# A two-block model's forward pass, in which the normalised columns get 1,280 bytes a k-tile and the weight tiles lie side by side

## The chip, the cores and the metric

The kernel runs on one core of one Trainium2 chip. The metric is the device time of one execution in microseconds (us), the median of several runs.

## What is computed

The input is 256 tokens of width 2,048. The first block has multi-head attention and a pooling branch, then a feed-forward part with a 3-tap convolution. The second block puts 16 learned tokens ahead, which makes 272 columns (`TOK`; `SEQ` is 256), and has two layers. The even layer multiplies the normalised tokens `u` by one wide matrix, and its parts feed a state-space scan and a 31-tap convolution; both results go through an output projection. The odd layer is neighbourhood attention with its own two projections. Cut to the lines around the change:

```python
h = x + jnp.concatenate([a, m], axis=-1) @ w_out       # block 1
h = h + conv_ffn(rms_norm(h, g), w_up, conv_w, conv_b, w_down)
u = rmsnorm(h, norm_g)                                 # even layer, 272 rows
proj = u @ w_in    # z_a, xs, B, C, dt_f, dt_b, z_b, glu_v, glu_g
y_a = ssd_mixer(...)
y_b = layernorm(conv31(glu_v * sigmoid(glu_g))) ...  * silu(z_b)
h = h + jnp.concatenate([y_a, y_b], axis=-1) @ w_out
u = rmsnorm(h, norm_g)                                 # odd layer
h = h + (neighbourhood_attention(q, k, v, rpb) * silu(z)) @ w_out
return rmsnorm(h, g)[:, 16:]
```

All products are in float32, each made from three fp32r products: weights and activations are split into a high and a low part, and high x high, high x low and low x high are added up in PSUM.

## The kernel before, in words

Activations lie transposed: a k-tile is 128 of the 2,048 features on the partitions by 272 (or 256) token columns. Weights stream from HBM in chunks of 512 KB: SyncE loads a chunk of eight 128 x 128 tiles into one of four `raw` buffers, ScalarE copies it as fp32r into `whi` (`split`, L680 and L682), VectorE or GpSimd subtracts and writes `wlo` (L1642, L1645, L620), and TensorE makes 24 matmuls of it (`product`, L1160 to L1177: three for each k-tile, at L1173, L1174 and L1175). Semaphores `hi_done`, `lo_done` and `chunk_done` count chunks. Each engine has its own program, whose order is written out by hand.

The stages by the name of their weights, with the activations that they read: `pin`, `qkv` and `up` read `th`/`tl` (256 columns, k-tiles 1,024 bytes apart), `mix` and `down` read `fh`/`fl` (the same); `dt`, `xbc`, `ssd` (with `ssd6` and `ssd7`) and `glu` read `xh`/`xl` (272 columns, k-tiles 1,088 bytes apart); `outa` reads `yah`/`yal` and `outb` `ybh`/`ybl` (272 columns, 1,088 bytes); `na` reads `xh`/`xl`, with 272 columns for values and keys and the last 256 for gate and queries; `naout` reads `oh`/`ol` (256 columns, 1,088 bytes apart). In the trace `xh`, `xl`, `th` and `tl` are all named `xhl`, `fh` and `fl` are `fhl`, `oh` and `ol` are `ohl`.

Two things are done about addresses within a partition. From `dt` on, the function `by_lines` (L1154) gives a matmul its columns in another order: four floats of every 64-byte line, then the next four of every line, on both the moving operand and the output. And from `dt` on, `spread` (L289) is true and the eight weight tiles of a chunk don't lie side by side: tile r starts at `r % 4 * GROUP + r // 4 * P` floats (L307), and `GROUP` is 272 floats, so that four pairs of tiles start 1,088 bytes apart, as the k-tiles of the activations do. Before `dt` the eight tiles lie side by side, 512 bytes apart, 64 bytes into the buffer.

Around the change: `rs` are two buffers for the reciprocal roots of the norms (`rs[0]` for `pin` to `qkv` and `dt` to `glu` and the last norm, `rs[1]` for `up` and `na`). `vec` holds all per-feature vectors, the 31-tap weights `conv31` among them; all but its first part are loaded by SyncE during `qkv` (L428). In `glu`, VectorE applies the 31 taps (L2278 to L2290) after the gate's and value's evacuations (L2269, L2270). GpSimd's queue has, before its splits of `glu` (L624), the clamps of the state-space stage and the loads `decay_rows` (L570).

Of the kernel before, what the change touches and what calls it, by code (L numbers as in the profile page):

```python
# [18 lines left out]
P = 128  # L19
D = 2048  # L20
KT = D // P
# [9 lines left out]
GROUP = 2 * P + LINE  # L31
WSLOT = 4 * GROUP
# [39 lines left out]
for _name, _n in (("g_attn", 16), ("g_q", 1), ("g_k", 1), ("rel", 8), ("pool_scale", 8),  # L72
                  ("g_ffn", 16), ("g_even", 16), ("g_odd", 16), ("g_final", 16),
                  ("g_ssd", 16), ("ffn_conv", FT * 8),
                  ("conv5", 32 * 6), ("conv31", 16 * 32), ("ln_g", 16), ("ln_b", 16), ("d_skip", 16),
                  ("dt_bias", 1), ("a_log", 1)):
    VECS[_name] = (_at, _n)
    _at += _n
NVEC = _at
NFIRST = VECS["g_ffn"][0]  # L80

# [32 lines left out]
def program(nc, io):  # L114
    ctx = ExitStack()
    with ctx:
# [27 lines left out]
        vec = at("vec", NVEC)  # L144
        ident = at("ident", P)
        ones = at("ones", P)
        tri = at("tri", 2 * DW, BF16)
        S0 = arena[0]
        sq = at("sq", 2 * TOK)
        nt = at("nt", TOK)  # L150
# [29 lines left out]
        pts = at("pts", 384, F32, U + 1536)  # L180
        sm = at("sm", 8, F32, U + 3072)
# [21 lines left out]
        pad5 = [at(f"pad5{n}", TOK + 4, F32, (s0 + 51712, s0 + 52832, s0 + 54016, U + 2624)[n]) for n in range(4)]  # L203
# [15 lines left out]
        lsq = at("lsq", 2 * TOK, F32, w + 15360)  # L219

        ohl = at("ohl", 2 * KT * TOK, F32R, Y)
        oh, ol = ohl[:, 0:KT * TOK], ohl[:, KT * TOK:2 * KT * TOK]
        cmask = at("cmask", 4 * 2 * NC, F32, w + 17536)
        n0 = Y + 34816
# [63 lines left out]

        def spread(phase, i, j):  # L289

            if isinstance(i, int):
                return chunk(phase, i, j) >= chunk("dt", 0, 0)
            return first(phase, 1) >= first("dt", 1)

        def tiles_of(t, spread_):

            if spread_:
                t = t[:, :].rearrange("p (q m) -> p q m", m=GROUP)[:, :, 0:2 * P]
                return t.rearrange("p q (h n) -> p h q n", n=P)
            return t[:, LINE:LINE + CW].rearrange("p (h q n) -> p h q n", h=2, n=P)  # L300

        def raw_tiles(t):
            return t[:, :].rearrange("p (h q n) -> p h q n", h=2, n=P)

        def wtile(t, r, spread_):

            o = r % 4 * GROUP + r // 4 * P if spread_ else LINE + r * P  # L307
            return t[:, o:o + P]
# [59 lines left out]
        def _(sp):  # L368
# [127 lines left out]
        def _(pool):  # L496
# [118 lines left out]
            def split(phase, i, j, lead=LEAD):  # L615
# [42 lines left out]
        def _(act):  # L658
# [14 lines left out]
            def split(phase, i, j, lead=LEAD):  # L673
# [1936 lines left out]
```

## Time and profile before

| | |
|---|---|
| median of 3 runs | 2375.08 us (2374.9 to 2377.41) |
| the profiled execution, its own time | 2376.99 us |
| its span, first to last instruction | 2375.2 us |
| TensorE matmuls, share of the span | 99%, 20,022 instructions |
| VectorE, ScalarE, GpSimd | 74%, 49%, 25% |
| granted TensorE clock | 0.998 of full speed, mean |
| DMA | 438.55 MB, mean 185 GB/s |

A matmul's recorded duration overlaps the next one's, so its mean tells little of the pace: what counts is how far apart the starts are. In a view by windows, the number after the x counts every instruction that overlaps the window. A matmul here lasts some 280 ns and starts are some 120 ns apart, so about 2.3 of the number were already running when the window began.

### The profile page before, as it was taken

How to read it: one execution, taken by the hardware profiler on the slowest of the kernel's cores; microseconds unless marked ns; L12 is line 12 of the kernel's file. 1: busy time of each engine (PE TensorE's matmuls, PEld its weight loads, DVE VectorE, ACT ScalarE, POOL GpSimd, SP SyncE). 2: the span in 40 equal slices, each digit the busy share in tenths (PEclk: the TensorE clock that was granted, in tenths of full speed). 3: DMA queues.
4: the chain of work that ended last, by engine and by line, in shares of the span. 5: the costliest groups of instructions: out<-in, count | busy, mean ns of one | idle time of the engine just before them, and what ended most of it. 6: DMA issues, size and time to landing. Idle time of an engine off the chain costs nothing.

```text
span 2375.2 us, 55946 instructions
## 1 busy us (share of the span) xinstructions
PE 2352.9 (99%) x20022; PEld 2322.0 (98%) x20022; DVE 1751.0 (74%) x3054; ACT 1173.6 (49%) x1647; POOL 582.4 (25%) x420
## 2 busy tenths in 40 slices
PE   8999999999999999999999999999999999999998
PEld 8999999999999999999999999999999999999997
DVE  6777877777777655589888878888872566666665
ACT  5444455555555444457666643333544444444453
POOL 0230000000000000013423368777777311111100
PEclk9999999999999999999999999999999999999999
DMA  8654666666666666656555545556555555555553
GB/s 281 212 165 143 207 200 200 203 201 201 199 205 197 201 194 195 190 181 198 177 181 169 181 161 177 175 173 192 176 174 175 187 175 161 171 166 177 164 170 133
DMA packets 152419, 438.55 MB, mean 185 GB/s; under 512 B 32324, under 2 KB 47213, under 8 KB 152189
## 3 DMA queue, kind: packets, MB, share of 16 engines
q1 hardware_dynamic: 148844, 424.68, 55.9%
q0 software_dynamic: 3184, 12.14, 1.8%
q8 instruction: 73, 1.20, 0.2%
q10 hardware_dynamic: 288, 0.30, 0.0%
q14 instruction: 30, 0.24, 0.0%
HBM read 434.88 MB, written 11.09 MB: 188 GB/s over the span
## 4 chain that ended last, share of the span: by engine, by line
PE 93%; DVE 4%; ACT 2%; issue 1%; DMA 0%; SPq 0%; DVEq 0%; ACTq 0%
PE bank L1175 29%; PE bank L1173 29%; PE bank L1174 29%; PE bank L1426 1%; DVE wlo L1642 1%; PE bank L1546 1%; PE bank L1536 1%; DVE c L2064 1%; PE bank L1526 1%; PE bank L1397 1%; DMA x<-x_tok 0%; ACT whi L682 0%; PE bank L1553 0%; PE bank L1271 0%; PE bank L1409 0%
## 5 line engine op out<-in xcount | busy, mean ns | idle before, releaser
L1173 PE MATMUL bank<-xhl,whi 128*128 128x256 f32 (+1 forms) x4494 | 1268.7, 282 | 1.2 <-DVE xhl L1713 1.2
L1175 PE MATMUL bank<-xhl,wlo 128*128 128x256 f32 (+1 forms) x4494 | 1261.8, 281 | 0.0
L1174 PE MATMUL bank<-xhl,whi 128*128 128x256 f32 (+1 forms) x4494 | 1257.6, 280 | 0.0
L1173 PEld LDWEIGHTS bank<-xhl,whi 128*128 128x128 f32 x4494 | 843.8, 188 | 4.1 <-DVE xhl L1713 1.5
L1174 PEld LDWEIGHTS bank<-xhl,whi 128*128 128x128 f32 x4494 | 845.8, 188 | 0.7 <-issue 0.2
L1175 PEld LDWEIGHTS bank<-xhl,wlo 128*128 128x128 f32 x4494 | 844.1, 188 | 0.0
L680 ACT CAST whi<-raw 128x1024 fp32r<-128x1024 f32 x420 | 438.7, 1046 | 372.7 <-PE bank L1175 361.9
L1645 DVE TENSOR_TENSOR wlo<-raw,whi 128x1024 fp32r<-128x1024 f32 x364 | 445.4, 1228 | 187.7 <-ACT whi L682 182.8
L682 ACT CAST whi<-raw 128x1024 fp32r<-128x1024 f32 x364 | 381.1, 1052 | 389.3 <-PE bank L1175 368.4
L620 POOL TENSOR_TENSOR wlo<-raw,whi 128x1024 fp32r<-128x1024 f32 x160 | 383.0, 2402 | 122.3 <-ACT whi L680 122.3
L1642 DVE TENSOR_TENSOR wlo<-raw,whi 128x1024 fp32r<-128x1024 f32 x260 | 319.1, 1228 | 108.6 <-ACT whi L680 105.7
L1173 PE MATMUL bank<-fhl,whi 128*128 128x256 f32 x960 | 265.9, 277 | 0.0
L1174 PE MATMUL bank<-fhl,whi 128*128 128x256 f32 x960 | 265.0, 276 | 0.0
L1175 PE MATMUL bank<-fhl,wlo 128*128 128x256 f32 x960 | 265.0, 276 | 0.0
L586 POOL MEMSET pad<- 128x2 f32 x4 | 0.3, 97 | 852.9 <-DVE dta L2019 852.9
L2288 DVE SCALAR_TENSOR_TENSOR bank<-u,vec,bank 128x272 f32<-128x272 f32 x448 | 187.4, 499 | 3.7 <-DVE zt L1656 3.7
L1174 PEld LDWEIGHTS bank<-fhl,whi 128*128 128x128 f32 x960 | 180.3, 188 | 0.0
L1173 PEld LDWEIGHTS bank<-fhl,whi 128*128 128x128 f32 x960 | 180.2, 188 | 0.0
L1175 PEld LDWEIGHTS bank<-fhl,wlo 128*128 128x128 f32 x960 | 180.2, 188 | 0.0
L580 POOL TENSOR_SCALAR ef<-bc,acsr 128x272 f32<-128x272 f32 (+2 forms) x90 | 93.9, 1055 | 175.0 <-PE bank L1426 171.3
L653 POOL TENSOR_TENSOR btm<-btr,cmask 128x160 f32<-128x160 f32 x64 | 46.7, 760 | 345.5 <-DVE nsc L2387 345.2
L695 ACT ACTIVATE sq<-x 128x272 f32 (+1 forms) x64 | 27.6, 432 | 144.0 <-DVE x L1898 144.0
(281 smaller groups left out, 2704.1 us busy)
## 6 DMA issues: line engine op xcount, KB each, us to landing
raw<-w_up SPq DMA_DIRECT2D x176, 512.0 KB, 4.4
raw<-w_na SPq DMA_DIRECT2D x128, 512.0 KB, 3.8
raw<-w_ssm SPq DMA_DIRECT2D x96, 512.0 KB, 3.9
raw<-w_glu SPq DMA_DIRECT2D x96, 512.0 KB, 3.6
raw<-w_down SPq DMA_DIRECT2D x80, 512.0 KB, 4.2
raw<-w_qkv SPq DMA_DIRECT2D x48, 512.0 KB, 4.5
raw<-w_mix SPq DMA_DIRECT2D x32, 512.0 KB, 4.2
raw<-w_outa SPq DMA_DIRECT2D x32, 512.0 KB, 3.8
```

What stands on the lines that cost most here:

```text
L580: ins = G.tensor_scalar(ef[k][0:rows, h * DW + o:h * DW + o + w_], bc[2 * k][0:rows, t0:t0 + w_], acsr[0:rows, c:c + 1], 0.0, SUB, ALU.min)
L620: nc.gpsimd.tensor_tensor(tiles_of(wlo[s], wide), raw_tiles(raw[s]), tiles_of(whi[s], wide).bitcast(F32), SUB).then_inc(sem("lo_done"), 1)
L653: ins = G.tensor_tensor(by_row(btm, (2 * h + b_) * NK, (4, 0)[b_], NC), from_, m_, ADD)
L680: A.copy(tiles_of(whi[s], True), raw_tiles(raw[s])).then_inc(sem("hi_done"), 1)
L682: A.copy(whi[s][:, LINE:LINE + CW], raw[s][:, :]).then_inc(sem("hi_done"), 1)
L695: A.activation(sq[:, k * TOK:k * TOK + TOK], src, ACT.Square).then_inc(sem("sq_done"), 1)
L1173: T.matmul(to_, wh, xh_, start=head, stop=False)
L1174: T.matmul(to_, wh, xl_, start=False, stop=False)
L1175: ins = T.matmul(to_, wl, xh_, start=False, stop=last)
L1642: V.tensor_tensor(tiles_of(wlo[s], True), raw_tiles(raw[s]), tiles_of(whi[s], True).bitcast(F32), SUB).then_inc(sem("lo_done"), 1)
L1645: V.tensor_tensor(wlo[s][:, LINE:LINE + CW], raw[s][:, :], whi[s][:, LINE:LINE + CW].bitcast(F32), SUB).then_inc(sem("lo_done"), 1)
L2288: ins = V.scalar_tensor_tensor(out=out, in0=src, scalar=c, in1=acc_, op0=MUL, op1=ADD)
```

## The change

- The k-tiles of `xh` and `xl` get 320 floats (1,280 bytes, `XW`) for their 272 columns, and both begin one line (64 bytes) into their part of `xhl`. `oh` and `ol` get 256 floats a k-tile instead of 272 and begin three lines in, as `th` and `tl` do. `yah`, `yal`, `ybh`, `ybl` stay as they are.
- `spread` and its helpers go; the eight weight tiles lie side by side in every stage. `by_lines` is applied in the same stages as before.
- To make room: `conv31` leaves `vec` and is loaded by GpSimd's queue into `taps31`, a buffer of its own over dead space of the scan stage, once the first bank of `ssd7` is free. VectorE waits for it ahead of the loop of `glu`. One buffer `rs[0]` serves all norms. `acc`, `nv`, `pts`, `sm` and `pad5[3]` move to other addresses.
- VectorE's residual of `down` has one loop of seven passes where a loop of six and a pass written out stood.

```diff
-GROUP = 2 * P + LINE
-WSLOT = 4 * GROUP
+XW = TOK + 3 * LINE
...
+NKEPT = VECS["conv31"][0]
...
-        rs = [at(f"rs{n}", TOK) for n in range(2)]
-        acc = at("acc", TOK)
-        whi = [at(f"whi{s}", WSLOT, F32R) for s in range(RING)]
-        wlo = [at(f"wlo{s}", WSLOT, F32R) for s in range(RING)]
-        nv = at("nv", TOK)
+        whi = [at(f"whi{s}", CW, F32R) for s in range(RING)]
+        wlo = [at(f"wlo{s}", CW, F32R) for s in range(RING)]
         x = at("x", KT * TOK)
-        xhl = at("xhl", 2 * KT * TOK, F32R)
-        xh, xl = xhl[:, 0:KT * TOK], xhl[:, KT * TOK:2 * KT * TOK]
+        xhl = at("xhl", 2 * KT * XW, F32R)
+        xh, xl = xhl[:, LINE:KT * XW], xhl[:, KT * XW + LINE:2 * KT * XW]
...
+        taps31 = at("taps31", 16 * 32, F32, w + 17536)
+
+        ohl = at("ohl", LINES + 2 * KT * SEQ, F32R, Y)
+        oh, ol = ohl[:, LINES:LINES + KT * SEQ], ohl[:, LINES + KT * SEQ:LINES + 2 * KT * SEQ]
...
-                    sp.dma_start(vec[:, NFIRST:NVEC], io["vecs"][:, NFIRST:NVEC]).then_inc(sem("vec_in2"), 16)
+                    sp.dma_start(vec[:, NFIRST:NKEPT], io["vecs"][:, NFIRST:NKEPT]).then_inc(sem("vec_in2"), 16)
...
+            pool.wait_ge(sem("bank_free"), tile("ssd7", 0, 0) + 3)
+            G.dma_start(taps31[:, :], io["vecs"][:, NKEPT:NVEC]).then_inc(sem("taps31_in"), 16)
             pool.wait_ge(sem("lo_done"), chunk("glu", 0, 0) + (LEAD + RING))
...
-                if spread(phase, i, j + lead):
-                    A.copy(tiles_of(whi[s], True), raw_tiles(raw[s])).then_inc(sem("hi_done"), 1)
-                else:
-                    A.copy(whi[s][:, LINE:LINE + CW], raw[s][:, :]).then_inc(sem("hi_done"), 1)
+                A.copy(whi[s][:, :], raw[s][:, :]).then_inc(sem("hi_done"), 1)
...
-                    wide = spread(phase, i, j)
-                    wh, wl = wtile(whi[s], r, wide), wtile(wlo[s], r, wide)
+                    wh, wl = whi[s][:, r * P:r * P + P], wlo[s][:, r * P:r * P + P]
...
-                product(phase, i, j, j // 2, xh, xl, ktiles(j), TOK, off, n, j % 2 == 0, j % 2 == 1)
+                product(phase, i, j, j // 2, xh, xl, ktiles(j), XW, off, n, j % 2 == 0, j % 2 == 1)
...
-                product("naout", 2, j, j // 2, oh, ol, ktiles(j), TOK, 0, SEQ, j % 2 == 0, j % 2 == 1)
+                product("naout", 2, j, j // 2, oh, ol, ktiles(j), SEQ, 0, SEQ, j % 2 == 0, j % 2 == 1)
...
-            norm(1, rs[1], EPS1)
+            norm(1, rs[0], EPS1)
...
+            dve.wait_ge(sem("taps31_in"), 16)
             with dve.Fori(0, 8) as i:
...
-                        src, c = u31[:, n:n + TOK], vcol("conv31", 32 * m + n, i, 64)
+                        src, c = u31[:, n:n + TOK], ncol(taps31, 32 * m + n, i, 64)
```

## Rows read from the trace of the kernel before

**Rows 1.** The page's part 4, the chain that ended last, by engine.
```profile
PE 93%; DVE 4%; ACT 2%; issue 1%; DMA 0%; SPq 0%; DVEq 0%; ACTq 0%
```
**Rows 2.** What TensorE waited for: us in total, times, longest; the latest-stage entry.
```profile
PE bank L1409 <- ACT cx L709: 1.1, 1, 1.1
```
**Rows 3.** TensorE by windows: us, busy (number), granted clock, DMA share, GB/s.
```profile
400.00:600.00 200.00, 200.00 (x1767) 1.00 0.63 203
...
1384.00:1419.00 35.00, 35.00 (x287) 1.00 0.56 181
1428.00:1660.00 232.00, 232.00 (x1859) 1.00 0.56 179
...
1701.00:1759.00 58.00, 58.00 (x466) 1.00 0.53 168
1761.00:1855.00 94.00, 94.00 (x754) 1.00 0.53 174
```
**Rows 4.** The same view, a window of naout.
```profile
2287.00:2350.00 63.00, 63.00 (x543) 1.00 0.55 175
```
**Rows 5.** TensorE's timeline in outa, 1679.7 to 1699.8 us: start, duration.
```profile
1679.73 0.29 PE L1174 MATMUL bank<-yal,whi 128*128 128x272 f32 x1
...
1699.74 0.28 PE L1175 MATMUL bank<-yah,wlo 128*128 128x272 f32 x1
```
**Rows 6.** TensorE's timeline in the ssd stage, 1157.7 to 1166.9 us.
```profile
1157.72 0.29 PE L1175 MATMUL bank<-xhl,wlo 128*128 128x272 f32 x1
...
1166.84 0.28 PE L1173 MATMUL bank<-xhl,whi 128*128 128x272 f32 x1
```
**Rows 7.** TensorE's timeline in na, a stretch of 272 columns.
```profile
2004.01 0.28 PE L1174 MATMUL bank<-xhl,whi 128*128 128x272 f32 x1
...
2011.24 0.28 PE L1173 MATMUL bank<-xhl,whi 128*128 128x272 f32 x1
```
**Rows 8.** TensorE's timeline in na, a stretch of 256 columns.
```profile
2017.74 0.27 PE L1174 MATMUL bank<-xhl,whi 128*128 128x256 f32 x1
...
2024.80 0.28 PE L1173 MATMUL bank<-xhl,whi 128*128 128x256 f32 x1
```
**Rows 9.** TensorE's timeline where the loop of glu begins.
```profile
1423.59 0.31 PE L1173 MATMUL bank<-xhl,whi 128*128 128x272 f32 x1
1423.74 0.28 PE L1174 MATMUL bank<-xhl,whi 128*128 128x272 f32 x1
```
**Rows 10.** Groups by line and shape on TensorE: number, busy us, mean ns.
```profile
L1173 PE MATMUL bank<-xhl,whi 128*128 128x272 f32 x2064 | 590.3, 286 | 0.0
...
L1173 PE MATMUL bank<-yah,whi 128*128 128x272 f32 x256 | 73.4, 287 | 0.0
...
L1173 PE MATMUL bank<-ybh,whi 128*128 128x272 f32 x256 | 73.1, 286 | 0.0
...
L1173 PE MATMUL bank<-ohl,whi 128*128 128x256 f32 x256 | 71.5, 279 | 0.0
```
**Rows 11.** The page's part 5: the splits of the weights.
```profile
L680 ACT CAST whi<-raw 128x1024 fp32r<-128x1024 f32 x420 | 438.7, 1046 | 372.7 <-PE bank L1175 361.9
L1645 DVE TENSOR_TENSOR wlo<-raw,whi 128x1024 fp32r<-128x1024 f32 x364 | 445.4, 1228 | 187.7 <-ACT whi L682 182.8
L682 ACT CAST whi<-raw 128x1024 fp32r<-128x1024 f32 x364 | 381.1, 1052 | 389.3 <-PE bank L1175 368.4
L620 POOL TENSOR_TENSOR wlo<-raw,whi 128x1024 fp32r<-128x1024 f32 x160 | 383.0, 2402 | 122.3 <-ACT whi L680 122.3
L1642 DVE TENSOR_TENSOR wlo<-raw,whi 128x1024 fp32r<-128x1024 f32 x260 | 319.1, 1228 | 108.6 <-ACT whi L680 105.7
```
**Rows 12.** The tile bc, which GpSimd's queue loads 32 times, 272 KB each.
```profile
DMA to landing us min/median/max: 3.6/5.1/8.7
```
**Rows 13.** VectorE's timeline between the first evacuation of ssd7 and glu.
```profile
1366.83 0.42 DVE L1656 TENSOR_TENSOR nv<-bank,rs 128x272 f32<-128x272 f32 x1
...
1382.89 0.28 DVE L2262 MEMSET bank<- 128x272 f32 x1
```
**Rows 14.** GpSimd's timeline there: its first split of glu's weights.
```profile
1377.77 2.38 POOL L620 TENSOR_TENSOR wlo<-raw,whi 128x1024 fp32r<-128x1024 f32 x1 [25.66 <-ACT whi L680]
```

More of the change, by code:

```diff
@@ L147, in program @@
         tri = at("tri", 2 * DW, BF16)
+        rs = [at("rs0", TOK)]
         S0 = arena[0]
         sq = at("sq", 2 * TOK)
+        acc = at("acc", TOK)
+        nv = at("nv", TOK)
         nt = at("nt", TOK)
@@ L202, in program @@
         dtc = at("dtc", TOK, F32, s0 + 50624)
-        pad5 = [at(f"pad5{n}", TOK + 4, F32, (s0 + 51712, s0 + 52832, s0 + 54016, U + 2624)[n]) for n in range(4)]
+        pad5 = [at(f"pad5{n}", TOK + 4, F32, (s0 + 51712, s0 + 52832, s0 + 54016, V0 + -(-VECS["ffn_conv"][0] // 8) * 32)[n]) for n in range(4)]
         ea = at("ea", 8, F32, s0 + 53952)
@@ L287, in wait_lo @@
             eng.wait_ge(sem("lo_done"), chunk(phase, i, j) + (1 + RING))
[L289 to L308, printed above, removed]
         class Chain:
@@ L741, in first_hi @@
                 act.wait_ge(sem(f"raw_in{j}"), 16)
-                A.copy(whi[j][:, LINE:LINE + CW], raw[j][:, :]).then_inc(sem("hi_done"), 1)
+                A.copy(whi[j][:, :], raw[j][:, :]).then_inc(sem("hi_done"), 1)
             def scaled_hi(q):
@@ L755, in _ @@
             act.wait_ge(sem("raw_first"), 16)
-            A.copy(whi[0][:, LINE:LINE + 2 * P], raw[0][:, 0:2 * P]).then_inc(sem("hi_first"), 1)
+            A.copy(whi[0][:, 0:2 * P], raw[0][:, 0:2 * P]).then_inc(sem("hi_first"), 1)
             act.wait_ge(sem("vec_in"), 16)
@@ L759, in _ @@
             act.wait_ge(sem("raw_in0"), 16)
-            A.copy(whi[0][:, LINE + 2 * P:LINE + CW], raw[0][:, 2 * P:CW]).then_inc(sem("hi_done"), 1)
+            A.copy(whi[0][:, 2 * P:CW], raw[0][:, 2 * P:CW]).then_inc(sem("hi_done"), 1)
             scaled_hi(1)
@@ L1152, in _, with by_lines @@
             pe.sem_inc(sem("chunk_done"), RING)
-            def by_lines(ap, wide):
-                if not wide:
+            def by_lines(ap, phase):
+                if ap.shape[-1] != TOK and phase not in ("na", "naout"):
                     return ap
@@ L1168, in product @@
                     r, o = kt % (4 if phase == "dt" else 8), kt * width + off
-                    wide = spread(phase, i, j)
-                    wh, wl = wtile(whi[s], r, wide), wtile(wlo[s], r, wide)
+                    wh, wl = whi[s][:, r * P:r * P + P], wlo[s][:, r * P:r * P + P]
                     head, last = start and n_ == 0, stop and n_ == len(kts) - 1
-                    to_, xh_, xl_ = (by_lines(a, wide) for a in (out, mh[:, o:o + n], ml[:, o:o + n]))
+                    to_, xh_, xl_ = (by_lines(a, phase) for a in (out, mh[:, o:o + n], ml[:, o:o + n]))
                     T.matmul(to_, wh, xh_, start=head, stop=False)
@@ L1579, in projecting @@
             def projecting(n, n_tile, kts, start=False, stop=False, done=True):
-                product("naout", n // 4, n % 4, n_tile % 2, oh, ol, kts, TOK, 0, SEQ, start, stop,
+                product("naout", n // 4, n % 4, n_tile % 2, oh, ol, kts, SEQ, 0, SEQ, start, stop,
                         {2: bank[2], 3: bank[3]}.get(n_tile), done)
@@ L1615, in last_products @@
                         T.matmul(bank[2][:, META:TOK], ones[:, :], acc[:, META:TOK], start=True, stop=False)
-                    product("naout", i, j, j // 2, oh, ol, ktiles(j), TOK, 0, SEQ, j % 2 == 0,
+                    product("naout", i, j, j // 2, oh, ol, ktiles(j), SEQ, 0, SEQ, j % 2 == 0,
                             j % 2 == 1)
@@ L1902, in landed @@
                     elif gain:
-                        both(tok(x, k, i, 2, 0, TOK), tok(xh, k, i, 2, 0, TOK),
-                             tok(xl, k, i, 2, 0, TOK), vcol(gain, k, i, 2)
+                        both(tok(x, k, i, 2, 0, TOK), tok(xh, k, i, 2, 0, TOK, XW),
+                             tok(xl, k, i, 2, 0, TOK, XW), vcol(gain, k, i, 2)
                              ).then_inc(sem("xs_ready"), 1)
@@ L1944, in residual @@
                     ch.end()
-                    with dve.Fori(1, 7) as i:
+                    with dve.Fori(1, 8) as i:
                         ch.begin(i, 2, 1)
                         body(i)
-                    ch.end(6)
-                    body(7)
-                    ch.end()
+                    ch.end(7)
                 else:
@@ L2279, in tap @@
                         out = c31[:, :] if n == TAPS - 2 else acc_
-                        src, c = u31[:, n:n + TOK], vcol("conv31", 32 * m + n, i, 64)
+                        src, c = u31[:, n:n + TOK], ncol(taps31, 32 * m + n, i, 64)
                         if n == 0:
-                            ins = V.tensor_scalar(out, src, c, vcol("conv31", 32 * m + TAPS, i, 64),
+                            ins = V.tensor_scalar(out, src, c, ncol(taps31, 32 * m + TAPS, i, 64),
                                                   MUL, ADD)
```

52 lines of the change are left out of this document (23 added, 29 removed).

## The prediction

> **What bounds the kernel.** I read the chain first: 93% of it is TensorE [rows 1]. Then TensorE's waits: the largest outside the kernel's start is 1.1 us [rows 2]. So the only thing that can move the time by much is how far apart the starts of the matmuls are, and a nanosecond there counts in full. The windows give that: the length over the number, less the 2.3 that were already running. With 256 columns in plain order (up) it is 200 / 1764.7 = 113.3 ns. With 272 columns it takes one of two values. The first part of glu has 35 / 284.7 = 122.9 ns, the rest of it 232 / 1856.7 = 125.0 ns, the rest of outa 58 / 463.7 = 125.1, outb 94 / 751.7 = 125.1 [rows 3]. The first part of outa has 163 starts in 20.01 us, 122.8 ns [rows 5]; one of three stretches of the scan stage with the same look has 73 in 9.12 us, 124.9 ns [rows 6], and na's 272 columns have 59 in 7.23 us, 122.5 ns [rows 7]. The clock is granted in full in all windows (1.00, the 2.4 GHz level), so it isn't the clock. It isn't the operands either: glu has both paces with the same tiles. The pace turns where something shakes the rhythm: at the entry of glu's loop two starts are 0.15 us apart instead of 0.12 [rows 9], and from there on the pace is the slow one; in outa it turns at an inserted matmul at 1,700 us. I call them the **quick** (122.8) and the **slow** (125.0) pace; they differ by 2.2 ns. In the 256-column stages with reordered columns there is such a spread too: na has 62 starts in 7.06 us, 113.9 ns [rows 8], naout 63 / 540.7 = 116.5 ns [rows 4].
>
> **What decides the pace** the trace doesn't show, but the addresses in the code offer one thing that the change alters: the distance between the moving k-tile and its weight tile, as a remainder by 256 bytes. I take 256 because four lines of 64 bytes is the step after which the old layout repeats. Before, weights begin at remainder 64 and step by 1,088 bytes, the columns at 128 and step by 1,088: the distance is 64 in every k-tile of xh, ya, yb and oh (for the second four weight tiles, 3,840 bytes off, also). For na's 256 columns, which begin 64 bytes later, it is 128; for th and fh it is 192.
>
> **The change, part by part.**
> 1. xh/xl (dt, xbc, ssd, glu, na). Weights now begin at 128 and step by 512, columns at 192 and step by 1,280: the difference of the steps is 768, three times 256. So the distance stays 64 (128 for na's 256 columns). All three matmuls of a k-tile see what they saw. Cost 0 on 3 x 2,064 matmuls of 272 columns [rows 10]. Bounds for what I can't see, that the places themselves matter: down to plain order's 113.3 x 272 / 256 = 120.4 ns, up to 125.0.
> 2. outa and outb, 2 x 768 matmuls (three lines of 256 each [rows 10]). Their columns keep 1,088 bytes, the weights now 512: the distance goes 0, 64, 128, 192 and round again. No row shows that. Bounds: the quick pace, 1,248 matmuls (156 us / 125.0 ns) x 2.2 ns = 2.7 us less; and, since the two 256-column stages that differ in distance and region differ most by 116.5 - 113.3 = 3.2 ns, 1,536 x 3.2 = 4.9 us more. I take 0: the stage already runs at the slow pace, and four distances in turn should average.
> 3. naout, 768 matmuls: from distance 64 to 192, in the same column order. Bounds: 113.3 (up, distance 192, plain order) and 116.5 (now). I take na's 113.9, the nearest in column order with a distance other than 64: 768 x 2.6 = **2.0 us less**.
> 4. The splits. ScalarE's copy takes 1,046 ns spread and 1,052 side by side, VectorE's subtraction 1,228 both ways [rows 11]: 0. GpSimd's takes 2,402 ns and has only the spread form; a chunk in glu lasts 24 x 125 = 3.0 us, and GpSimd waits for ScalarE between splits [rows 11], so 0.6 us more each would be hidden, and less is worth nothing.
> 5. The 31-tap weights. SyncE's load in qkv shrinks by 256 KB; nothing on the path waits for it: 0. GpSimd issues a load of 256 KB after the evacuation that ends at 1366.83 + 0.42 = 1367.3 us; its queue's 272 KB loads land in 5.1 us, at worst 8.7 [rows 12]: at 1372.4, worst 1376.0. VectorE comes to the new wait at 1382.89 + 0.28 = 1383.2 [rows 13]. Slack 7.2 us at worst, cost 0. Behind the load on GpSimd's queue stands its first split, at 1377.77 after 25.66 us of idling [rows 14]: also free. If the cover were gone, behind VectorE's wait stand glu's first evacuations, for which TensorE's banks wait.
> 6. One `rs`: VectorE writes it and reads it in its own order, and no other engine reads it: 0. The moved buffers and the loop of seven passes issue the same instructions: 0.
>
> Sum: -2.0 us. The profiled execution's own time is 2376.99 us for a span of 2375.2, 1.9 above the median, 2375.1; so 2375.0 for that execution and **2373.1 us** for the median. A measurement of this kernel can tell some 0.2%, 4.8 us, from no change, so this is no difference.
>
> **The rivals.**
> - **No place matters.** Then naout keeps 116.5 ns and the median stays 2375.1. For it: glu has both paces with the same addresses. Against: na and naout differ by 2.6 ns in one column order. The Trainium skill, "SBUF — State Buffer", section "Who interferes with whom", is on this side: TensorE has two independent read ports, one for moving columns and one for weights, and never waits on anyone. By it the whole change would be worth nothing; the trace, with 122.9 and 125.0 ns in one stage, shows at least that something unnamed there takes time.
> - **glu falls into the quick pace.** Which pace follows a shake seems to hang on the moment it comes at: in the scan stage three stretches are slow and the others quick. glu from 1423.9 to 1663.5 us is 239.6 us / 125.0 = 1,917 matmuls x 2.2 = 4.2 us less, with naout 6.2: 2368.9. Against: addresses by remainder, order and shake are as before, so the same turn should follow.
> - **The fixed place is better.** Every k-tile of xh now begins at the same remainder, where before it walked by 64 bytes. If that takes the whole 272-column work in xh from about 123.7 on average to between 122.3 and 120.4 ns, 6,192 matmuls give 9 to 20 us: some 2363, with naout. For it: outb's gaps repeat after 12 matmuls, four k-tiles, which is the walk's own length. Against: glu's slow pace repeats after 3 and the quick one after 9, which a walk of 12 would break (these repeats are in the starts to the nanosecond; the printed rows round to ten).
> - **The slow pace spreads** (the side of slower). What now runs quick in xh, about 2,050 of the scan stage, 1,536 of na and 320 of glu, is some 3,900 matmuls; at the slow pace that is 8.6 us more, less naout's 2.0: 2381.7. It decides from about 3,070 such matmuls on (6.8 us, which leaves 4.8 net). For it: every interruption draws anew, and na has two in each of 16 passes. Against: the distances are unchanged, and na's passes all look alike now.
> - **The round of distances in outa and outb** costs its bound of 4.9 us and naout doesn't gain: 2380.0. The late load of the taps is worth a chance of 0.01 only.
>
> **How the numbers follow.** Forecast with no visible difference 0.39 (0.26 as summed, 0.13 no place matters). Faster 0.37: glu quick 0.20, fixed place 0.17. Slower 0.24: slow pace 0.16, outa and outb 0.07, taps 0.01. The range goes down to 2361 (part of the fixed place's 20 us is left out, about 0.08) and up to 2383 (2381.7 and a little; about 0.08 left out, where mishaps add up). The likeliest case's own range is 2370.5 to 2376.
>
> **What would show it.** Right: TensorE still at 93% or so of the chain; up at 113.3 ns; windows in ssd and na at 122.8 and 113.9; glu after its loop's entry at 125.0; naout at 113.9 instead of 116.5; outa and outb between 123 and 127, with gaps that repeat after 12; no wait of VectorE for `taps31`, landed by 1,376 us. Wrong: glu at 122.8 throughout (second rival), any xh stage under 122.5 (third), ssd or na at 125 (fourth), outa and outb over 127, or naout still at 116 or above; and a median under 2370 or over 2380 makes the sum wrong, whichever stage it comes from.

## The result, and the profile after

The changed kernel takes 2361.11 us (median of 4 runs, 2360.02 to 2361.49), the one before 2375.77 (4 runs, 2374.9 to 2377.41): a ratio of 0.9936, 95% interval 0.9923 to 0.995. It is faster by 14.7 us, where 2.0 had been summed, and lies at the very end of the stated range of 2361 to 2383. The two profiled executions stand a little further apart, 17.0 us by their spans (2375.2 and 2358.2 us): the one before lies 1.2 us above its median, the one after, 2360.02 us, 1.1 below.

**Where it went, by stage.** The tile view gives the first and last start of each stage's matmuls. Kernel before:

```profile
L1173 PE MATMUL bank<-fhl,whi x960: 276/276/470, 217.0 to 1026.0; 128*128 128x256 f32 x192
L1426 PE MATMUL bank<-ef,xr x192: 179/286/443, 1085.2 to 1378.3; 128*64 128x272 f32 x64, 128*64 128x144 f32 x64, 128*64 128x16 f32 x64
L1173 PE MATMUL bank<-yah,whi x256: 279/285/485, 1663.9 to 1759.9; 128*128 128x272 f32 x128
L1173 PE MATMUL bank<-ybh,whi x256: 284/286/287, 1760.3 to 1855.9; 128*128 128x272 f32 x128
L1173 PE MATMUL bank<-ohl,whi x256: 274/276/464, 2268.3 to 2362.2; 128*128 128x256 f32 x128
```

Changed kernel, the same view (its lines 1151, 1152 and 1153 are 1173, 1174 and 1175 of before):

```profile
L1151 PE MATMUL bank<-fhl,whi x960: 276/276/470, 217.0 to 1026.0; 128*128 128x256 f32 x192
L1404 PE MATMUL bank<-ef,xr x192: 179/286/443, 1085.0 to 1374.1; 128*64 128x272 f32 x64, 128*64 128x144 f32 x64, 128*64 128x16 f32 x64
L1151 PE MATMUL bank<-yah,whi x256: 280/283/483, 1652.5 to 1747.9; 128*128 128x272 f32 x128
L1151 PE MATMUL bank<-ybh,whi x256: 282/283/382, 1748.3 to 1842.8; 128*128 128x272 f32 x128
L1151 PE MATMUL bank<-ohl,whi x256: 271/277/466, 2252.8 to 2345.2; 128*128 128x256 f32 x128
```

Up to 1026.0 us nothing has moved. From there each stage's length is the difference of two rows (scan stage with dt and xbc to 1378.3, glu to 1663.9, and so on; na from the last start of ybh to the first of ohl, outa and outb likewise):

| | dt to ssd7 | glu | outa | outb | na | naout, end |
|---|---|---|---|---|---|---|
| before, us | 352.3 | 285.6 | 96.4 | 95.6 | 412.4 | 106.9 |
| after, us | 348.1 | 278.4 | 95.8 | 94.5 | 410.0 | 105.4 |
| difference | -4.2 | -7.2 | -0.6 | -1.1 | -2.4 | -1.5 |

So 13.8 of the 17.0 us are in the three stages that read `xh`, which the prediction had put at nothing.

**The pace.** Windows of TensorE (us, busy with the number of instructions, granted clock, DMA share, GB/s):

```profile
400.00:600.00 200.00, 200.00 (x1767) 1.00 0.63 202
1560.00:1592.00 32.00, 32.00 (x269) 1.00 0.55 180
...
1700.00:1740.00 40.00, 40.00 (x327) 1.00 0.49 162
1750.00:1840.00 90.00, 90.00 (x731) 1.00 0.55 180
2275.00:2335.00 60.00, 60.00 (x527) 1.00 0.57 184
```

Less the 2.3 instructions already running, `up` has 200 / 1764.7 = 113.3 ns as before, a stretch within one pass of glu 32 / 266.7 = **120.0 ns** (125.0 before [rows 3]), outa 123.2, outb 90 / 728.7 = 123.5 (125.1 before; this window holds a stop of 0.1 us, and the undisturbed starts are 123.3 apart), naout 60 / 524.7 = 114.4 (116.5 [rows 4]). The clock is 1.00 in all, the 2.4 GHz level. Na's two shapes, from TensorE's timeline:

```profile
2002.58 0.28 PE L1151 MATMUL bank<-xhl,whi 128*128 128x256 f32 x1
...
2010.74 0.27 PE L1153 MATMUL bank<-xhl,wlo 128*128 128x256 f32 x1
...
2014.47 0.28 PE L1151 MATMUL bank<-xhl,whi 128*128 128x272 f32 x1
...
2023.02 0.28 PE L1153 MATMUL bank<-xhl,wlo 128*128 128x272 f32 x1
```

Each stretch has 72 starts. With 272 columns they are 8.55 / 71 = 120.4 ns apart (122.5 before [rows 7]), with 256 columns 8.16 / 71 = 114.9 ns (113.9 before [rows 8]): 1 ns dearer, which gives back 1.5 of the 3.7 us that na's 272 columns gain (1,536 matmuls of each shape; 122.8 and 120.4 ns by the means of the whole stage). The old rhythm is gone too. In glu the starts before were 128, 125 and 122 ns apart in turn; now 1,898 of 2,265 undisturbed starts are 120 ns apart to the nanosecond, and most of the others lie in a stretch of about one pass that runs at 122.2. So glu's mean is 120.4, and 120.0 is the settled pace.

**A new wait in glu.** The chain says that TensorE is no longer alone: by engine it was 93% and 4% [rows 1], now

```profile
PE 87%; DVE 7%; issue 3%; ACT 2%; DMA 1%; DVEq 1%; SPq 0%; ACTq 0%
```

and the waits of TensorE in glu have an entry that was not there (total us, times, longest):

```profile
PE bank L1151 <- DVE gt L1630: 0.9, 6, 0.2
```

TensorE's timeline at the seam between two passes of glu's loop:

```profile
1523.61 0.28 PE L1153 MATMUL bank<-xhl,wlo 128*128 128x272 f32 x1
1524.04 0.38 PE L1151 MATMUL bank<-xhl,whi 128*128 128x272 f32 x1 [0.15 <-DVE gt L1630]
1524.26 0.28 PE L1152 MATMUL bank<-xhl,whi 128*128 128x272 f32 x1
```

and the chain over the same seam:

```profile
1522.52 0.45 DVE zb L2274
1523.13 0.23 issue
1523.47 0.45 DVE gt L1630
1524.04 0.38 PE bank L1151
```

Two starts are 0.43 and 0.22 us apart instead of 0.12: TensorE waits for a bank that VectorE evacuates (`gt`) only when it is through with the taps of the pass before. From 1488.59 us on the stops are at 1488.59, 1523.61, 1558.63, 1593.66 and 1628.64, so a pass takes 35.02 us, where 288 matmuls at 120.0 ns would take 34.56 and took 36.0 before (288 x 125.0). About 0.45 us of such a pass's gain of 1.44 is lost at its seam, some 2.7 us at the six seams that have this wait.

The sum over the three stages shows the same. By the mean distances of undisturbed starts, the pace alone gave 6.2 us in the scan stage (2,376 matmuls, 123.1 to 120.5 ns), 9.7 in glu (2,287, 124.6 to 120.4) and 3.7 less 1.5 in na, 18.1 together. The stages became 13.8 us shorter. Of the other 4.3, 2.5 were lost in glu, mostly at its seams, and 2.0 in the scan stage (na came out 0.2 better), where TensorE's printed waits grew from 1.1 us [rows 2] to 2.0:

```profile
PE bank L1387 <- ACT cx L688: 1.4, 1, 1.4
PE bank L1387 <- DVE cbm L2048: 0.4, 1, 0.4
PE bank L1375 <- ACT cx L688: 0.2, 1, 0.2
```

### The profile page after: what moved, and what is told of

Its sections match the earlier page's. It is cut to its first block, busy times and chain, and to the rows that moved or that the text cites. A ratio compares the mean times of both kernels' runs of the same rounds, so it can differ in the third digit from the quotient of the medians.

```text
span 2358.2 us, 55982 instructions
## 1 busy us (share of the span) xinstructions
PE 2334.5 (99%) x20022; PEld 2302.0 (98%) x20022; DVE 1748.6 (74%) x3054; ACT 1173.1 (50%) x1647; POOL 582.6 (25%) x421
## 4 chain that ended last, share of the span: by engine, by line
PE 87%; DVE 7%; issue 3%; ACT 2%; DMA 1%; DVEq 1%; SPq 0%; ACTq 0%
PE bank L1151 27%; PE bank L1152 27%; PE bank L1153 27%; DVE bank L2261 1%; DVE wlo L1619 1%; DVE c L2036 1%; PE bank L1404 1%; ACT whi L661 1%; PE bank L1524 1%; DMA raw<-w_p 1%; DMA raw<-w_qkv 1%; PE bank L1514 1%; PE bank L1504 1%; PE bank L1375 1%; PE bank L1531 0%
## 5 line engine op out<-in xcount | busy, mean ns | idle before, releaser
L661 ACT CAST whi<-raw 128x1024 fp32r<-128x1024 f32 x784 | 819.6, 1049 | 740.6 <-PE bank L1153 706.7
L1619 DVE TENSOR_TENSOR wlo<-raw,whi 128x1024 fp32r<-128x1024 f32 x624 | 764.9, 1229 | 292.3 <-ACT whi L661 285.3
L600 POOL TENSOR_TENSOR wlo<-raw,whi 128x1024 fp32r<-128x1024 f32 x160 | 381.2, 2391 | 98.8 <-ACT whi L661 98.6
L2261 DVE SCALAR_TENSOR_TENSOR bank<-u,taps,bank 128x272 f32<-128x272 f32 x448 | 187.5, 501 | 3.7 <-DVE zt L1630 3.7
L1872 DVE TENSOR_TENSOR x<-bank,x 128x256 f32 (+2 forms) x64 | 27.3, 426 | 80.7 <-PE bank L1153 80.7
L2036 DVE SCALAR_TENSOR_TENSOR c<-pad,vec,c 128x272 f32<-128x272 f32 x128 | 67.6, 528 | 9.0 <-DVE c L2036 0.6
```

The lines of the kernel that those rows point to most:

```text
L600: nc.gpsimd.tensor_tensor(wlo[s][:, :], raw[s][:, :], whi[s][:, :].bitcast(F32), SUB).then_inc(sem("lo_done"), 1)
L661: A.copy(whi[s][:, :], raw[s][:, :]).then_inc(sem("hi_done"), 1)
L1619: V.tensor_tensor(wlo[s][:, :], raw[s][:, :], whi[s][:, :].bitcast(F32), SUB).then_inc(sem("lo_done"), 1)
L1872: freed(phase, i, k, V.tensor_tensor(xt, from_[:, 0:n], xt, ADD))
L2036: ins = V.scalar_tensor_tensor(out=c5[q][:, :], in0=pad5[q][:, n:n + TOK], scalar=vslot("conv5", S, 24, 24 + 6 * q + n), in1=c5[q][:, :], ...
L2261: ins = V.scalar_tensor_tensor(out=out, in0=src, scalar=c, in1=acc_, op0=MUL, op1=ADD)
```

## The experiments

All are edits of the changed kernel and compute the same sums; e7, e11 and e15 add them up in another order. The ratios are to the kernel before, run beside each group of experiments. "Distance" is, as in the prediction, the address of the streamed columns less that of a weight tile, modulo 256 bytes. M1, M2 and M3 are the three matmuls of a k-tile: high weights by `xh`, high weights by `xl`, low weights by `xh`. The paces in the tables are the mean distance of undisturbed starts over a whole stage, worked out from the trace's starts. Each kernel was profiled once, and its rhythms can differ between executions: the kernel before took 2370.27 to 2378.9 us in the 25 runs beside e13 to e15, the changed kernel 2360.02 to 2361.49 in its four.

What made me look again at "the distance stays" is this pair of rows of the changed kernel, weight loads (PEld) and matmuls in one stretch:

```profile
1499.85 0.28 PE L1153 MATMUL bank<-xhl,wlo 128*128 128x272 f32 x1
...
1499.85 0.19 PEld L1151 LDWEIGHTS bank<-xhl,whi 128*128 128x128 f32 x1
```

The weight load that starts with a matmul is that of the **next** one (it lasts 0.19 us, so it also reaches into its own matmul, which starts 0.12 us later). Beside M1 the same high tile is loaded again, beside M2 the low tile of the same k-tile, beside M3 the high tile of the next k-tile. In the kernel before, where weights and columns both step by 1,088 bytes (64 modulo 256), M1 and M2 see 64, and M3 sees 64 - 64 = 0. In the changed kernel both steps are 0 modulo 256, and M3 sees 64 as well. **Theory F:** what counts is this distance, and 0 is dear. **Theory A:** it is the walk itself, columns and weights that begin at another remainder in each k-tile.

### The other parts of the change

**e1_squeezes.** The layouts of before (columns, spread weights, `oh`) and its loop of six in `down`, with the rest of the change: the late taps, the single `rs`, the moved buffers.

```diff
-XW = TOK + 3 * LINE
+XW = TOK
+GROUP = 2 * P + LINE
...
+            o = r % 4 * GROUP + r // 4 * P if spread_ else LINE + r * P
...
-                    with dve.Fori(1, 8) as i:
+                    with dve.Fori(1, 7) as i:
```

> Only the room-making parts of the change: taps31 loaded late, one buffer for the roots, the moved buffers. Weights spread and columns every 1,088 bytes as before. If the paces alone made the gain: 2375 us, glu 122.8 then 125.0 ns, na 122.8 and 113.9, naout 116.5. If the late load or the moved buffers had a part in it: below 2373.

Measured: 2374.78 us against 2374.61, 1.000 (0.999 to 1.001). The late taps, the single `rs` and the moved buffers are worth nothing. The loop of seven was not run by itself; it lies in `down`, whose last matmul starts at 1026.0 us with it and without. In e1's profile glu keeps the quick pace of 122.8 ns until about 1,600 us and is slow only behind that,

```profile
1480.00:1640.00 160.00, 160.00 (x1300) 1.00 0.55 177
```

160 / 1297.7 = 123.3 ns instead of 125.0, with the same distances as before. So the layout doesn't settle which of the two old rhythms a pass falls into, as the second rival had it. The profiled execution, 2373.76 us, is 3.2 us quicker than the profiled one of before, and the median did not move.

**e4_shift64.** Everything behind `raw` 64 bytes further, all distances kept.

```diff
+        arena[0] += 64
         whi = [at(f"whi{s}", CW, F32R) for s in range(RING)]
```

> The changed kernel with every buffer behind raw 64 bytes further on: distances and steps the same, every place moved by one line. If only steps and distances count: 120.0, 114.8 and 114.4 ns stay, 2361 us. If the remainder of the place itself counts: xh's stages or na's 256 columns change by 1 to 3 ns, so 2355 to 2380 us, and up may leave 113.3 ns too.

Measured: 2361.38 us, 0.9942 (0.9925 to 0.9959), and the same number of matmuls in the window as the changed kernel (x1316 in both):

```profile
1480.00:1640.00 160.00, 159.57 (x1316) 1.00 0.56 181
```

The absolute place is not what counts.

### Walk or distance

**e2_step576.** As e1, but weight tiles at equal steps of 576 bytes, so that they walk without coming in pairs.

```diff
...
-            o = r % 4 * GROUP + r // 4 * P if spread_ else LINE + r * P
+            o = r * WT if spread_ else LINE + r * P     # WT = P + LINE
```

> As the last kernel, but each weight tile starts 576 bytes after the one before (1,088 - 512). The distance of columns and weights is the same in every k-tile to any power of two, and both still walk by 64 bytes. Theory A (it is the walk that costs): paces as before, 2375 us. Theory B (it is the spread layout, whose distance jumps by 3,840 bytes, an odd multiple of 256, at the fifth tile): 120.0 ns in xh's stages and in outa and outb too, some 2350 us.

Measured: 2376.38 us, 1.0006 (0.9997 to 1.0016). Scan stage 122.9, glu 123.8, outb 125.0 ns. The form of the spread does not matter as long as both walk by 64.

**e3_side_only.** Weights side by side, columns still 1,088 bytes a k-tile, so that own and next distances go through all four values in every stage.

```diff
-XW = TOK + 3 * LINE
+XW = TOK
...
-        xh, xl = xhl[:, LINE:KT * XW], xhl[:, KT * XW + LINE:2 * KT * XW]
+        xh, xl = xhl[:, LINE:LINE + KT * XW], xhl[:, LINE + KT * XW:LINE + 2 * KT * XW]
```

> As the changed kernel, but the columns of xh and xl every 1,088 bytes: the weights side by side alone, and the distance goes round 64, 128, 192, 0. Theory A (walk) and theory C (the distance must hold): xh's stages as outa and outb are in the changed kernel, 123.3 ns, 2.9 ns x 6,192 = 18 us more, 2379 us. Theory D (weights side by side are quicker by themselves): 120.0 ns stays, 2361 us.

Measured: 2372.68 us, 0.999 (0.9981 to 1.0): 123.0 in the scan stage, 123.3 in glu. The paces are those of theories A and C in the expectation, but the time is 6 us under their 2379. Side-by-side weights alone bring a sixth or so (0.1% of the 0.64%); the padding of the columns, which keeps the distance at 64 everywhere, is what brings the rest. The changed kernel's outa and outb are in this state: 123.2 and 123.3.

**e5_distance128** and **e9_distance0.** Nothing walks; `xh` and `xl` begin two lines, or none, into their parts.

```diff
-        xh, xl = xhl[:, LINE:KT * XW], xhl[:, KT * XW + LINE:2 * KT * XW]
+        xh, xl = xhl[:, 2 * LINE:KT * XW], xhl[:, KT * XW + 2 * LINE:2 * KT * XW]     # e5
+        xh, xl = xhl[:, 0 * LINE:KT * XW], xhl[:, KT * XW + 0 * LINE:2 * KT * XW]     # e9
```

> The changed kernel with xh and xl one line further on: the distance is 128 instead of 64 for 272 columns, 192 instead of 128 for na's 256; columns and weights stay fixed. Theory A (only the walk of the columns counts): 120.0 ns stays in all xh stages, 2361 us. Theory C (the distance counts, and 64 is a good one): xh's 272 columns at 121 to 124 ns, 2367 to 2385 us.

> The changed kernel with xh and xl one line further back: distance 0 in all three matmuls of a k-tile (64 for na's 256 columns). Theory F (the weights of the next matmul are read while this one streams, so in a walking layout the third matmul of a k-tile sees distance 64 - 64 = 0): distance 0 is dear, 126 ns or more in xh's stages, since it has to lift the mean of 120, 120 and itself to 122.8 or more; 2390 us or more. If distance 0 costs 123 ns or less, theory F does not add up.

Measured: e5 2368.78 us, 0.9966 (0.9954 to 0.9979); e9 2388.84 us (2 runs), 1.0055 (1.0035 to 1.0075), a little under the 2390 expected. Glu of e5:

```profile
1480.00:1640.00 160.00, 160.00 (x1306) 1.00 0.54 177
```

and of e9:

```profile
1480.00:1640.00 160.00, 160.00 (x1265) 1.00 0.53 173
```

160 / 1303.7 = 122.7 and 160 / 1262.7 = **126.7 ns**. A fixed place is not enough, as theory A would have it: the same padding costs 120.0, 122.7 or 126.7 ns, by where the columns begin. At 2.4 GHz the distance from 120.0 to 126.7 is 16 cycles a matmul. Distance 0 is dear in the other stages too, though less so: 125.2 ns in the scan stage and 124.7 for na's 272 columns.

**e6_step1152.** Columns of 1,152 bytes a k-tile, weights side by side: the distance is 64 and 192 in turn.

```diff
-XW = TOK + 3 * LINE
+XW = TOK + LINE
```

> The changed kernel with 1,152 bytes a k-tile instead of 1,280: the columns alternate between two places 128 bytes apart. If the remainder by 128 is what must hold: 120.0 ns, 2361 us. If it is the remainder by 256: the pace of outa and outb or of the kernel before, 122.8 ns or more, 2378 us.

Measured: 2370.22 us, 0.9974 (0.9964 to 0.9985), 122.3 ns in glu. Neither of the two expectations came, the pace lies between them. With half of the k-tiles at 64 and half at 192 the settled 120.0 ns is gone.

**e14_distance192.** The fourth place.

```diff
+        xh, xl = xhl[:, 3 * LINE:KT * XW], xhl[:, KT * XW + 3 * LINE:2 * KT * XW]
```

> Changed kernel with xh and xl 128 bytes further, distance 192 in every matmul of 272 columns (0 in na's 256 columns). It fills the map, which has 126.7 ns at 0, 120.0 at 64, 122.2 to 123.3 at 128. Theory F in the form that only the size of the distance counts either way (192 is 64 behind): 120.0 ns and, with na's 256 columns at 0 costing up to 1.5 us, 2361 to 2363 us. Theory F in the form that the price rises from 64 on to 256: 123.5 to 125 ns, 2373 to 2380 us. Theory A: 120.0 ns.

Measured: 2369.33 us (10 runs) against 2377.35 (25 runs), 0.9974 (0.9965 to 0.9984). Glu:

```profile
1480.00:1640.00 160.00, 160.00 (x1305) 1.00 0.55 177
```

160 / 1302.7 = 122.8 ns. Both forms of theory F that I had written down miss: the price is neither the same for 64 ahead and 64 behind (120.0), nor does it rise towards 256 (123.5 to 125). And na's 256 columns, at distance 0 here, are not dear but cheap. With the runs above the map for a fixed place is

| distance | 0 | 64 | 128 | 192 |
|---|---|---|---|---|
| 272 columns in glu, ns | 126.6 (e9) | 120.4 (after) | 122.5 (e5) | 122.6 (e14) |
| 256 columns in na, ns | 114.1 (e14) | 115.9 (e9) | 114.8 (after) | 114.4 (e5) |

Of these four, the best distance of one shape is the worst of the other. Naout points the same way: 116.5 ns at 64 (with M3 at 0, since it walked before), 114.4 at 192.

### Which of the three matmuls

**e10_xl_only** and **e13_xl_distance0.** Only `xl` moves: M2 sees 128, or 0; M1 and M3 stay at 64 and nothing walks.

```diff
+        xh, xl = xhl[:, LINE:KT * XW], xhl[:, KT * XW + 2 * LINE:2 * KT * XW]     # e10
+        xh, xl = xhl[:, LINE:KT * XW], xhl[:, KT * XW:2 * KT * XW]                # e13
```

> The changed kernel with xl alone one line further on: only the second matmul of a k-tile streams at distance 128, the first and third at 64. Theory F, with 122.5 ns measured for distance 128 in all three: (120.0 + 122.5 + 120.0) / 3 = 120.8 ns, 2366 us. If the places have to agree in all: 122.5 ns, 2373 us.

> Changed kernel, but xl begins 64 bytes earlier than there, so that the second matmul of each k-tile streams columns at distance 0 from the low weights that it has loaded for the third; the first and the third stay at 64, nothing walks. Theory F (distance 0 between the streamed columns and the weights being loaded is dear, wherever in the k-tile it falls): one of three at 0, as the third is in the walking layouts, so their pace, 122.2 to 125.0 ns in ssd and glu instead of 120.4, and 2373 us (2369 to 2377). Theory A (the walk itself costs): nothing walks, 120.0 to 120.5 ns and 2361 us. Had distance 0 no special price beside another uneven distance, it would be as with xl at 128: 122.2 ns, 2368.7 us.

Measured: e10 2368.72 us, 0.9974 (0.996 to 0.9987), 122.2 ns; e13 2371.52 us (10 runs) against 2377.35, 0.9981 (0.9971 to 0.9991). Glu of e10:

```profile
1480.00:1640.00 160.00, 160.00 (x1307) 1.00 0.54 177
```

and of e13:

```profile
1480.00:1640.00 160.00, 160.00 (x1303) 1.00 0.54 178
```

160 / 1304.7 = 122.6 and 160 / 1300.7 = **123.0 ns**. e13 speaks against theory A most directly: nothing walks, one matmul of three is at 0, and the pace is that of the kernel before, 122.9 ns, down to a repeat after nine matmuls, here within a nanosecond. The time is within the range expected. The price is not a sum over the three matmuls: one of them off its place costs 1.8 ns on all (122.2 for 120.4), three at 128 hardly more (122.5). In M1 and M2 the distances to the own and to the next weights are the same, so e10 and e13 don't tell which of the two counts.

**e11_walk_paired** and **e15_backwards.** The layout of e2, where both walk and the distance to the own weights is 64 in every matmul. Only the order of a chunk's eight k-tiles is changed, and with it what M3 sees: 64 and 0 in turn, or always 128.

```diff
+                if spread(phase, i, j) and len(kts) == 8 and phase != "naout":
+                    kts = [kts[n] for n in (0, 4, 1, 5, 2, 6, 3, 7)]     # e11
+                    kts = kts[::-1]                                      # e15
```

> The layout with 576-byte steps (columns and weights walk together), but each chunk of the stages from xbc to na takes its k-tiles in the order 0, 4, 1, 5, 2, 6, 3, 7: four of eight k-tiles are now followed by one at the same remainder, so only half of the third matmuls see distance 0. Theory F: half of the way from 122.8-125.0 to 120.0, some 121.4 to 122.5 ns in xbc to outb, 2362 us. Theory A (each place for itself costs): as the 576 layout, 2376 us.

> The layout of the run with steps of 576 and 1,088 bytes (both walk, own distance 64), but each chunk's eight k-tiles are multiplied in the reverse order. The third matmul of a k-tile then streams at distance 128 from the next k-tile's weights instead of 0. Theory F: as with one of three at 128, 122.2 to 122.5 ns in glu, outa and outb (there 123.8, 124.2, 125.0) and some 122.4 in ssd: 2376.4 less 1.0 (ssd), 2.5 (glu), 3.6 (outa, outb), 1.0 (na), about 2368.5 us. Theory A (walking costs) and the theory that only the distance to the matmul's own weights counts: the same walk and the same own distances, 2376.4 us.

Measured: e11 2364.89 us, 0.9957 (0.9941 to 0.9973); e15 2374.34 us (10 runs) against 2377.35, 0.999 (0.9981 to 1.0).

| ns | dt to ssd7 | glu | outa | outb | na, 272 columns |
|---|---|---|---|---|---|
| e2, M3 at 0 | 122.9 | 123.8 | 124.2 | 125.0 | 122.8 |
| e15, M3 at 128 | 122.4 | 123.3 | 123.9 | 123.9 | 123.8 |
| e11, M3 at 64 and 0 | 121.5 | 120.7 | 123.1 | 121.5 | 121.8 |

Outb of e2 (the second window of a kernel, 90 us of one unbroken pace):

```profile
1750.00:1840.00 90.00, 90.00 (x722) 1.00 0.56 183
```

Outb of e15 and of e11:

```profile
1750.00:1840.00 90.00, 90.00 (x727) 1.00 0.57 182
```

```profile
1750.00:1840.00 90.00, 89.90 (x740) 1.00 0.57 184
```

90 / 719.7 = 125.1, 90 / 724.7 = 124.2 and 90 / 737.7 = 122.0 ns (the last two windows hold a stop of some 0.2 and 0.4 us near their start; the table leaves it out). The own distances are 64 in all three, and the same tiles are multiplied; what differs is which tile comes next. That settles that the distance to the own weights is not all that counts: at the same own distances outb takes 125.0 or 121.5 ns.

Whether it is the next weights or the walk needs both runs. In e11 the columns also change their remainder half as often, so e11 alone fits a theory in which each such change costs. In e15 they change as often as in e2, and both rhythms lie 1.1 ns lower (121.7 and 123.9 for 122.8 and 125.0). So the weights loaded ahead take part. The size of e15 is a miss: I had expected 122.2 to 122.5 throughout and some 8 us, not 2 to 3, and 1.0 us less in na, whose 272 columns became 1.0 ns dearer instead, since in e15's profile they fall into the higher of the two rhythms and in e2's into the lower. One matmul at 128 is dearer as M3 of a walk than as M2 of a fixed layout, and why stays open. No run has M3 alone at 0 with nothing walking, so how much of the old pace is M3's distance and how much the walk is not shown.

**e7_paired.** The same order of pairs in outa and outb of the changed kernel, where weights don't walk and the columns do.

```diff
+            def paired(j):
+                return [j % 2 * 8 + n for n in (0, 4, 1, 5, 2, 6, 3, 7)]
...
-                    product("outb", i, j, j // 2, ybh, ybl, ktiles(j), TOK, 0, TOK, j % 2 == 0,
+                    product("outb", i, j, j // 2, ybh, ybl, paired(j), TOK, 0, TOK, j % 2 == 0,
```

> The changed kernel, but outa and outb take the eight k-tiles of a chunk in the order 0, 4, 1, 5, 2, 6, 3, 7: the columns change their remainder four times a chunk instead of eight. Theory A (each change of place costs, about 3 x 3.3 = 10 ns): outa and outb go from 123.3 to about 121.7 ns, 2.5 us less, 2358.6 us. If the walk's cost is something else: 123.3 ns stays.

Measured: 2360.81 us, 0.9935 (0.9918 to 0.9951), 123.2 ns in both, as before the edit. Here half the own distances are still 0 and 192, and turning two neighbours into equals buys nothing.

### The columns' order, and a faster version

**e8_plain256.** The 256-column matmuls of na and naout in plain order.

```diff
-                if ap.shape[-1] != TOK and phase not in ("na", "naout"):
+                if ap.shape[-1] != TOK:
```

> The changed kernel, but the 256-column matmuls of na and naout take their columns in plain order. If the reordering is what costs there: 113.3 ns as in up, (1.5 x 1,536 + 1.1 x 768) = 3.1 us less, 2358.0 us. If their distance (128 in na) needs the reordering: na's 256 columns over 115 ns, 2361 us or more; naout, at up's distance of 192, goes to 113.3 in both.

Measured: 2370.36 us, 0.9976 (0.9965 to 0.9986): 119.9 ns in na (114.8), and in naout 117.2 by the starts, where `up` in the same plain order has 113.3:

```profile
2275.00:2335.00 60.00, 60.00 (x513) 1.00 0.56 184
```

So plain order is no floor, and `up`'s 113.3 was no guide to naout, though both are at distance 192 in the changed kernel. The reordering is worth some 9 us.

**e12_yb_padded.** `ybh` and `ybl` too get 1,280 bytes a k-tile and begin one line in (`zb` and `uc`, whose space they share, likewise; other buffers of glu move).

```diff
-        ybh = at("ybh", KT * TOK, F32R, Y + 52224)
-        ybl = at("ybl", KT * TOK, F32R, Y + 34816)
+        ybh = at("ybh", KT * XW - 3 * LINE, F32R, Y + 55296 + 64)
+        ybl = at("ybl", KT * XW - 3 * LINE, F32R, Y + 34816 + 64)
...
```

> The changed kernel with uc, zb, ybh and ybl at 1,280 bytes a k-tile too, one line in, so that outb has distance 64 fixed; the small buffers of glu and outa moved together to make room. Theories A and F: outb from 123.35 to 120.0-120.5 ns, 768 x 3 = 2.3 us less, 2358.8 us; outa as it was. If something else than the layout holds outb back: 123.3 ns stays, 2361 us.

Measured: 2358.84 us (2357.68 to 2359.5), 0.9928 (0.9912 to 0.9945). Outb:

```profile
1750.00:1840.00 90.00, 90.00 (x738) 1.00 0.54 178
```

90 / 735.7 = 122.3 ns where the changed kernel has 123.5. It settled in a rhythm of 122.2 that repeats after nine and nearly after three, which the changed kernel's glu also shows for a pass, and not in the 120.0 that I had expected; the time came out as expected all the same. It is the fastest version, 2.3 us below the changed kernel by the medians, though the two intervals overlap and the difference was not measured side by side. The same for `yah` and `yal` was not tried: I found no room for it beside the scan stage's buffers.

## Why the prediction was wrong, point by point

- **What bounds the kernel** held: the pace of the matmuls, at full clock, decides. That the rest would stay hidden did not quite hold: at 120.0 ns VectorE's pass of glu is not covered any more.
- **Step 1 failed**, in the sentences "So the distance stays 64 ... All three matmuls of a k-tile see what they saw. Cost 0." It took the distance of each matmul to its own weights alone. The weights whose load starts with a matmul are the next ones, and at M3 these are the next k-tile's: at 0 before, at 64 after. What it put at 0 was worth 13.8 us, 18.1 by the pace of the starts. That own distances are not enough is shown by e11 and e2 (121.5 and 125.0 ns at the same ones), that distance 0 is dearer than 64 without any walk by e13 and e9 (122.9 and 126.6 ns in glu, for 120.4). How the gain divides between M3's distance and the walk stays open. The rows for it were at hand, since the trace of before shows weight loads and matmuls side by side. With that step the prediction's own premise, that the distance decides, would have pointed at a change in one matmul of three in 6,192. Its lower bound of 120.4 ns was close to what came (120.0 settled, 120.4 to 120.5 over a stage), though taken from plain order, which has nothing to do with it.
- **The third rival**, "the fixed place is better", came nearest: some 2363 for 2361.11. Part of that is luck: its own bounds, 9 to 20 us and naout's 2.0, give 2364 to 2353, the pace gained as much as its far end has it (123.6 to 120.4 ns in xh's 272 columns), and the stops and na's 256 columns took a third back. Its ground, that a fixed place is better in itself, does not hold: nothing walks in e5, e9, e13 and e14, and their glu takes 122.5 to 126.6 ns. Its argument against, that glu's rhythm repeats after 3 and 9, weighed too much: M3 is at 0 in every k-tile, walk or not, which is just what repeats after 3.
- **Step 2** took 0 with bounds of -2.7 and +4.9; measured -1.7 by the rows above. Four distances in turn run at 123.2 and 123.3, near the quick pace.
- **Step 3** took 113.9 ns and 2.0 us for naout; 114.4 and 1.5. It was right by luck in part: the value came from na's 256 columns at 128, which cost 114.8 once nothing walks.
- **Not seen:** that na's 256 columns change too, +1.0 ns, 1.5 us. Their distance to the next weights changed with everything else's.
- **Step 4** held. The splits, from the page's costliest groups of the changed kernel:

```profile
L661 ACT CAST whi<-raw 128x1024 fp32r<-128x1024 f32 x784 | 819.6, 1049 | 740.6 <-PE bank L1153 706.7
L1619 DVE TENSOR_TENSOR wlo<-raw,whi 128x1024 fp32r<-128x1024 f32 x624 | 764.9, 1229 | 292.3 <-ACT whi L661 285.3
...
L600 POOL TENSOR_TENSOR wlo<-raw,whi 128x1024 fp32r<-128x1024 f32 x160 | 381.2, 2391 | 98.8 <-ACT whi L661 98.6
```

  1,049, 1,229 and 2,391 ns, for 1,046 to 1,052, 1,228 and 2,402 [rows 11].
- **Step 5** held with room. The load is issued at 1363.7 us, after the evacuation of ssd7, and lands in 3.0 us (the page had 3.6 to 8.7 for its neighbours [rows 12]), at 1366.7; VectorE is at its wait at 1378.67 + 0.28 = 1378.95, 12.3 us later, and the idle time before its next instruction is put down to its own MEMSET. From the tile view of the taps, the DMA view and VectorE's timeline:

```profile
L605 POOL DMA_DIRECT2D taps<-vecs x1: 599/599/599, 1363.7 to 1363.7; - x1
```

```profile
taps<-vecs POOLq DMA_DIRECT2D x1, 256.0 KB, 3.0
```

```profile
1378.67 0.28 DVE L2234 MEMSET bank<- 128x272 f32 x1
1379.18 0.44 DVE L1630 TENSOR_TENSOR gt<-bank,rs 128x272 f32<-128x272 f32 x1 [0.22 <-DVE bank L2234]
```

- **Step 6** held for the single `rs` and the moved buffers, and step 5 with it, in e1: 1.000. E1 has the old splits and the old loop, so it says nothing of step 4 or of the loop of seven.
- **No place matters**, and with it the rule of the Trainium skill ("SBUF — State Buffer", section "Who interferes with whom") that TensorE's two read ports are independent and that it waits on no one, would have given no difference. The runs speak against that conclusion: 120.0 to 126.7 ns for the same instructions, by an offset of 64 bytes in where the columns begin. Whether it is the ports that collide or something else that goes by the address, no trace shows.
- **Quick glu** did not come about in the changed kernel, but e1 shows that it can: 123.3 for 125.0 in one execution, with no gain in the median. The slow pace's spread did not come.

## What to carry to other kernels

Where TensorE is back to back, its pace is a quantity to measure for each stage, to a nanosecond, and the layout of both operands is a knob: here 64 bytes, in where the columns begin, moved 272-column matmuls between 120.0 and 126.7 ns, 1.2% of the kernel's time. When two accesses are said to meet, write down which ones are under way at the same moment: the weights of the next matmul count too, so the seam between k-tiles has to be looked at as well as the matmul's own pair. The best offset is one of a shape and is to be tried for each shape, and after every gain on the bounding engine the loop's second engine has to be looked at again, as with VectorE in glu, where a pass is now 35.02 us for 34.56 of matmuls.

## What the runs showed of the hardware

- Starts of 272-column fp32r matmuls settle at one of a few paces, with equal gaps at 120.0 ns (all three matmuls at 64) and 126.7 ns (all at 0), and unequal ones at 122.2, 122.8 and 125.0 that repeat after 9, 9, and 3 or 12. One layout can show two of them (120.0 and 122.2; 122.8 and 125.0), and the profiles show the turn at a loop's seam or an inserted matmul.
- For 256 columns the order of the distances is another one: 114.1 ns at 0, 115.9 at 64, 114.8 at 128, 114.4 at 192 in the reordered form (113.8 in e10, with M2 at 192 and the others at 128). In plain order it is 113.3 in `up`, 117.2 in naout and 119.9 in na, the last two with the same instruction and other addresses.
- Open: how the old pace divides between the distance to the next weights and the walk, why the price of a single matmul off its place spreads over all three, why 256 columns behave otherwise, and what the remainder by 256 bytes stands for. That 256 is the period was not tried by itself; e4, where all moves together, and the pairs of the old layout, 3,840 bytes apart, are only in keeping with it.
